# A two-layer streaming trunk on one core: the pair preparation of layer 1 with the value projection one pair ahead

## What is computed

```python
k = xk @ w_k
v = xv @ w_v
kk = heads(k * k_k)
kk = kk / jnp.maximum(jnp.sqrt(jnp.sum(kk * kk, axis=-1, keepdims=True)), L2_EPS)
k_mod = k.astype(f32) * (1.0 + (a - 1.0) * k_a.astype(f32))
b_h = kk * a_h
# the scan over tokens uses r, decay, k_mod, v, kk and b; afterwards
o = o + (jnp.sum(r_h * k_h * r_k, axis=-1, keepdims=True) * v_h).reshape(B, T, D_MODEL)
```

## Time and profile before

| What | us |
|---|---|
| median of the three runs (4078.36 to 4090.19) | 4087.38 |
| the profiled execution | 4082.8 |
| its span, first to last instruction | 4081.0 |
| the pair stage in it: last key tile read (2153.4) to L1932 (2350.0) | 196.6 |

### The profile page before, as it was taken

The page is one execution under the profiler, slowest core; times in us unless marked ns, Lnnn a source line. Parts: engine busy times, 40 slices in busy tenths (PEclk is TensorE's granted clock), DMA queues, the critical chain, the costliest instruction groups (busy, mean ns, idle before and its releaser), DMA issues.

```text
span 4081.0 us, 65997 instructions
## 1 busy us (share of the span) xinstructions
PE 3684.9 (90%) x28466; PEld 3299.1 (81%) x28466; DVE 1534.3 (38%) x2023; ACT 853.4 (21%) x1132; POOL 206.8 (5%) x347
## 2 busy tenths in 40 slices
PE   6999999799999998968997768888698999999977
PEld 4997348699999997844996657777497999999967
DVE  3134544522212224431337734454625221222352
ACT  2001322300000001133324423333422000001020
POOL 0000000000000000000002111111100000000000
PEclk8999999899999999986998878898899999999989
DMA  2222011111121131112325732121412112112111
GB/s 88 67 68 79 21 42 71 65 47 41 57 75 47 42 128 39 39 61 109 113 86 217 269 107 54 43 54 29 145 37 75 41 40 76 63 41 99 66 37 70
DMA packets 75366, 300.53 MB, mean 74 GB/s; under 512 B 9400, under 2 KB 11720, under 8 KB 71160
## 3 DMA queue, kind: packets, MB, share of 16 engines
q0 software_dynamic: 36816, 174.51, 11.7%
q1 hardware_dynamic: 38336, 122.87, 9.6%
HBM read 216.24 MB, written 81.10 MB: 73 GB/s over the span
## 4 chain that ended last, share of the span: by engine, by line
PE 72%; DVE 8%; issue 2%; ACT 2%; DMA 1%; POOL 0%; DVEq 0%; ACTq 0%; POOLq 0%
PE ps L447 54%; PE ps L421 3%; DVE A L1470 2%; PE ps L856 2%; PE ps L847 2%; PE ps L757 1%; DVE B L1470 1%; PE ps L461 1%; PE ps L807 1%; DVE H L1551 1%; DVE A_r L1527 1%; PE ps L870 1%; PE ps L873 1%; PE ps L479 1%; PE ps L822 1%
## 5 line engine op out<-in xcount | busy, mean ns | idle before, releaser
L447 PE MATMUL ps<-H_r,W_r 128*128 128x364 f32 (+1 forms) x3192 | 705.2, 329 | 0.0
L447 PE MATMUL ps<-H_r,TM_r 128*128 128x364 f32 x2736 | 606.7, 330 | 21.7 <-DVE A_r L1527 18.2
L447 PE MATMUL ps<-A_r,TM_r 128*128 128x364 f32 x2736 | 606.2, 330 | 0.0
L447 PEld LDWEIGHTS ps<-H_r,W_r 128*128 128x128 f32 (+1 forms) x3192 | 555.9, 188 | 1.8
L447 PEld LDWEIGHTS ps<-H_r,TM_r 128*128 128x128 f32 x2736 | 475.1, 189 | 28.2 <-issue 19.8
L447 PEld LDWEIGHTS ps<-A_r,TM_r 128*128 128x128 f32 x2736 | 476.8, 189 | 0.0
L447 PE MATMUL ps<-B_r,DW_r 128*128 128x364 f32 x2112 | 408.9, 329 | 0.0
L447 PE MATMUL ps<-B_r,W_r 128*128 128x364 f32 x1824 | 405.0, 330 | 0.0
L447 PEld LDWEIGHTS ps<-B_r,DW_r 128*128 128x128 f32 x2112 | 358.8, 188 | 0.0
L447 PEld LDWEIGHTS ps<-B_r,W_r 128*128 128x128 f32 x1824 | 319.7, 190 | 0.0
L1733 DVE TENSOR_TENSOR TM<-ps,TM 128x1092 f32<-128x1092 f32 x44 | 57.0, 1296 | 444.4 <-PE ps L447 444.4
(11 more groups left out here) (288 smaller groups left out, 4390.2 us busy)
## 6 DMA issues: line engine op xcount, KB each, us to landing
W<-in_wgu SPq DMA_DIRECT2D x88, 512.0 KB, 3.6
H<-d_h POOLq DMA_DIRECT2D x3, 4368.0 KB, 23.0
W<-in_wdown SPq DMA_DIRECT2D x32, 384.0 KB, 3.1
W<-in_wrkv SPq DMA_DIRECT2D x24, 512.0 KB, 3.6
W<-in_wdown SPq DMA_DIRECT2D x32, 320.0 KB, 2.9
d_h<-H POOLq DMA_DIRECT2D x16, 546.0 KB, 3.0
d_y<-TM POOLq DMA_DIRECT2D x16, 546.0 KB, 3.4
A<-d_y POOLq DMA_DIRECT2D x16, 546.0 KB, 7.9
```

The lines of the kernel that those rows point to most:

```text
L447: ins = nc.tensor.matmul(ps[0:cols, NCH * s + c, 0:CH], w[:, j * cols:(j + 1) * cols], x[k1][:, c * CH:(c + 1) * CH], start=(k1 == 0 and n ...
```

## The change

The pair loop is written out (it was a loop of two times four pairs), and five things in it differ.

1. TensorE runs V one pair ahead: V(0), then for each pair A(p), V(p+1), R(p).
2. ScalarE squares the next key (`key_square(pair + 1)`, which waits for that pair's four loads) and then takes V(p+1) out of PSUM (`value_tile(pair + 1)`), and then R(p).
3. The upper part of the value weights is made by ScalarE (`upper_value`), two pairs ahead; VectorE only subtracts (`lower_value`). The scaling by `ka` moves to ScalarE as well, into `tmpK`.
4. VectorE's clamp of A(p) is gone: the logarithm reads PSUM directly with a tiny bias, and the normed key takes a minimum with 1/L2_EPS. The scaling of the log decay is folded into the scale of the exponentials.
5. GpSimd stores v one pair ahead: `keep_value(0)`, then in iteration p `keep_value(p + 1)` ahead of the store of the sum.

The core of the diff:

```diff
-                    sums(k("pair"), TM[:, 1, :])
-                    split_unit(xh, xlow[1])
-                    pe.wait_ge(S["rk_ready"], t.up("rk_ready"))
-                    sums(k("pair"), TM[:, 2, :])
+            split_unit(xh, xlow[1], arriving=True)
+            for pair in range(NPAIR):
+                pe.wait_ge(S["key_sq"], pair + 1)
+                sums(k("pair"), TM[:, 1, :])
+                if pair + 1 < NPAIR:
+                    split_unit(xh, xlow[1])
+                pe.wait_ge(S["rk_ready"], pair + 1)
+                sums(k("pair"), TM[:, 2, :])
...
+            def key_square(pair):
+                key, L = key2[pair % 2], Lb[pair % 2]
+                if pair >= 2:
+                    act.wait_ge(S["pair_done"], pair - 1)
+                act.wait_ge(S[f"l_in{pair % 2}"], t.up(f"l_in{pair % 2}", 64))
+                nc.scalar.activation(key, L["k"], ACT.Copy, scale=v1("kk", pair)).then_inc(S["key_scaled"], 1)
+                act.wait_ge(S["key_scaled"], pair + 1)
+                nc.scalar.activation(TM[:, 1, :], key, ACT.Square).then_inc(S["key_sq"], 1)
...
+            upper_value()
+            upper_value()
+            key_square(0)
+            value_tile(0)
+            for pair in range(NPAIR):
...
+                nc.scalar.activation(tmpK, L["a"], ACT.Identity, scale=v1("ka", pair),
+                                     bias=kab[:, pair:pair + 1]).then_inc(S["k_scale"], 1)
...
+                nc.scalar.activation(c3(TM[:, 3, :]), pset(s), ACT.Ln, bias=eps[:, 2:3]).then_inc(S[f"read{s}"], 1)
...
+                nc.scalar.activation(L["w"], L["w"], ACT.Exp, scale=-DECAY).then_inc(S["act_p"], 1)
+                if pair + 2 < NPAIR:
+                    upper_value()
+                if pair + 1 < NPAIR:
+                    key_square(pair + 1)
+                    value_tile(pair + 1)
+                s, mm, rd = t.unit()
+                act.wait_ge(S["mm_done"], mm)
+                nc.scalar.activation(c3(TM[:, 2, :]), pset(s), ACT.Copy).then_inc(S[f"read{s}"], 1)
...
+                nc.vector.tensor_tensor_scan(cumL, reset, L["w"], 0.0, ALU.mult, ALU.add).then_inc(S["dve_p"], 1)
+                nc.vector.tensor_tensor(L["w"], cumL, L["w"], ALU.subtract).then_inc(S["dve_p"], 1)
+                nc.vector.tensor_tensor(L["k"], tmpK, L["k"], ALU.mult).then_inc(S["k_used"], 1)
+                stt(TM[:, 2, :], L["r"], v1("rk", pair), L["k"], ALU.mult, ALU.mult).then_inc(S["rk_ready"], 1)
+                stt(key, TM[:, 3, :], 1.0 / L2_EPS, key, ALU.min, ALU.mult).then_inc(S["rn_used"], 1)
...
+            keep_value(0)
+            for i in range(NPAIR):
+                t.skip(1)
+                if i + 1 < NPAIR:
+                    keep_value(i + 1)
                 s, mm, rd = t.unit()
                 pool.wait_ge(S[f"read{s}"], rd)
                 pool.dma_start(d_x["sum"][i], TM[:, 2, :]).then_inc(S["sum_out"], 16)
```

More of the change, by code:

```diff
@@ L55 @@
 DECAY = float(np.exp(-0.5))
+TINY = 1e-34
 SUMS = 8
@@ L315, in build_trunk @@
[L315 to L318, removed]
@@ L1313, in _ @@
             act.wait_ge(S["xn_ready"], t.val("xn_tmp"))
[L1314 to L1349, removed]
@@ new lines, in lower_value @@
+            def lower_value(pair):
+                slot, landed = t.chunk()
+                dve.wait_ge(S["vh_ready"], pair + 1)
+                nc.vector.tensor_tensor(Wr[:, slot, 0:KT * P], W[:, slot, 0:KT * P], wh_of(t),
+                                        ALU.subtract).then_inc(S["wl_ready"], 1)
+                t.up("wl_ready")
+            tmpK = DWf[:, 0:T]
+            lower_value(0)
+            lower_value(1)
+            for pair in range(NPAIR):
+                key, L = key2[pair % 2], Lb[pair % 2]
+                dve.wait_ge(S[f"l_in{pair % 2}"], t.up(f"l_in{pair % 2}", 64))
+                nc.vector.tensor_tensor_scan(cumL, reset, L["w"], 0.0, ALU.mult, ALU.add).then_inc(S["dve_p"], 1)
+                dve.wait_ge(S["dve_p"], t.up("dve_p"))
+                nc.vector.tensor_tensor(L["w"], cumL, L["w"], ALU.subtract).then_inc(S["dve_p"], 1)
+                t.up("dve_p")
+                dve.wait_ge(S["k_scale"], pair + 1)
+                dve.wait_ge(S["key_scaled"], pair + 1)
+                nc.vector.tensor_tensor(L["k"], tmpK, L["k"], ALU.mult).then_inc(S["k_used"], 1)
+                dve.wait_ge(S["k_used"], pair + 1)
+                dve.wait_ge(S["sum_stored"], t.up("sum_stored"))
+                stt(TM[:, 2, :], L["r"], v1("rk", pair), L["k"], ALU.mult, ALU.mult).then_inc(S["rk_ready"], 1)
+                t.up("rk_ready")
+                dve.wait_ge(S["key_rn"], t.up("key_rn"))
+                stt(key, TM[:, 3, :], 1.0 / L2_EPS, key, ALU.min, ALU.mult).then_inc(S["rn_used"], 1)
+                dve.wait_ge(S["rn_used"], t.up("rn_used"))
+                step(nc.vector.tensor_tensor(tmpA, key, L["a"], ALU.mult))
+                dve.wait_ge(S["pair_stored"], t.up("pair_stored"))
+                dve.wait_ge(S["act_p"], t.up("act_p", 2))
+                for dst, x, y in zip(chunks(ar_out, o=C), tokens(L["r"]), tokens(expL)):
+                    nc.vector.tensor_tensor(dst, x, y, ALU.mult)
+                for dst, x, y in zip(chunks(bk_out), tokens(tmpA), tokens(expnL)):
+                    nc.vector.tensor_tensor(dst, x, y, ALU.mult)
+                for dst, x, y in zip(chunks(bk_out, o=C), tokens(L["k"]), tokens(expnL)):
+                    nc.vector.tensor_tensor(dst, x, y, ALU.mult)
+                dve.wait_ge(S["act_p"], t.up("act_p"))
+                if pair + 2 < NPAIR:
+                    lower_value(pair + 2)
+                for dst, x, y in zip(chunks(ar_out), tokens(key), tokens(L["w"])):
+                    ins = stt(dst, x, -1.0, y, ALU.mult, ALU.mult)
+                ins.then_inc(S["pair_done"], 1)
+                dve.wait_ge(S["pair_done"], t.up("pair_done"))
@@ L2231, in _, with keep_value @@
             pool.sem_inc(S["pair_stored"], 1)
-            for i in range(NPAIR):
-                t.skip(1)
+            def keep_value(i):
                 s, mm, rd = t.unit()
```

103 lines of the change are left out of this document (47 added, 56 removed).

## The result

The changed kernel takes 4065.46 us (median; 4060.14 to 4069.30) against 4087.55 of the kernel before beside it (4078.36 to 4092.07): ratio 0.9947, 95% interval 0.993 to 0.9963. It is 22 us faster; 9 us slower was predicted.

A forecast was written before the change was run, and what follows sets the result against it. TensorE's chain bounds the pair stage now, 21.17 us per pair; after the change, load landings gate it: 2217 + 5 × 22.6 = 2330, plus 29.0 gives L1932 at 2359, +9 on 4087.4 = 4096 us; range 4082 to 4108.

The forecast's parts named there:

- the sum: Whole kernel: L1932 starts at 2359 against 2350.0, so +9 us on 4082.8, or 4096 us against the median.
- The case "faster": Pair stage: loads in before ScalarE asks, TensorE sets the pace at 15.7 us a pair, −41 us, 4046; chance 0.08.
- The cycle: Pair stage: one pair's load landing gates issue of the next pair's loads; 8.9 us plus d_bk's issue to last landing.
- the waits named as signs: Pair stage: ScalarE waits longest for loads, TensorE about 5 us ahead of A, VectorE for `pair_stored`; d_bk to d_bk 22 to 24.
- The start of the cycle: Pair stage entry: d_bk(0) at 2204, pair 2's loads landed 13 later at 2217, against 2209.5 today.
- X: Pair stage: time from d_bk's issue to the last load's landing, taken as 13.7 us; 13.0 without the weight load.
- the period: Pair stage: time from one pair's load landing to the next's, 22.6 us, 1.4 more than today; bounds 21.9 and 24.7.
- the weight load's hour: Pair stage: weight load issued 7.5 to 8.1 us after a pair's loads land (L), ahead of d_bk at L + 8.9.
- The first rival: Pair stage: weight load still collides in full, period 24.0 to 24.7, +16 to +19 us, 4103 to 4106; chance 0.32.
- The end: Pair stage's end: after pair 7's loads land no further load follows; L1932 starts 29.0 us after that landing.
- The work taken off VectorE: Pair stage: clamp, scaling and cast leave VectorE, some 3.0 to 3.4 us a pair; booked as zero gain.
- The offer of 40 us: Pair stage: TensorE's 21.2 us a pair less 15.7 of work, 5.5 a pair, some 40 us if nothing else becomes late.

The follow-up runs named there:

- experiments 1 and 3: Kernel before with only TensorE's pair loop written out, 4039.09 us; kernel before with 128 unused semaphore increments on TensorE between pair stage and scan, 4032.78 us.
- Experiment 4: Changed kernel with ScalarE squaring the next key after taking V of the next pair and R out of PSUM: 4042.09 us, ratio 0.9909.
- experiment 10: Changed kernel with the key's load put ahead of the stores d_bk and d_ar, with its own semaphore that the squared key waits for: 4031.21 us, ratio 0.9880.
- Experiment 7: Changed kernel with SyncE holding each weight load of the pair stage until a pair's loads have landed: 4052.64 us, ratio 0.9947.
- experiment 12: Changed kernel with the key loaded first, plus 221 unused semaphore increments on TensorE between the stages: 4023.01 us, ratio 0.9856.

## Why the prediction was wrong, point by point

- **The step that failed is the sum.** "+9 us on the profiled execution's 4082.8" carries everything outside the pair stage over unchanged, without a reason given. It was not: the scan gave back 44.7 us, and experiments 1 and 3 show that this came from the number of TensorE instructions ahead of it, with the pair stage as before: the stops for instructions fell from 24 to 6, and the time at the lower clock from 92 to 24 us. No rival named it. The case "faster", 0.08, had another mechanism that did not happen.
- **The cycle was right.** The landing of one pair's loads gates the issue of the next pair's; the waits named as signs are those of the changed kernel (d_bk to d_bk is 24.2 us, just above the 22 to 24 named). Experiment 4 takes the key from ahead of the tiles and 19.4 of the 20.7 us are gone; experiment 10 leaves the order and lets the key land early, and the stage falls below that of before.
- **The start of the cycle was right.** d_bk(0) was put at 2204; it is issued at 2210.12, in a stage that began 5.7 later. Pair 2's loads landed at 2224.0, so 2218.3 counted from the old start, where 2217 was said.
- **X was mis-sized,** 13.7 against 15.0, and with it the period, 22.6 against 24.3. The forecast called the weight load's hour rightly (L + 7.9, 1.0 us ahead of d_bk) and took that for half out of the way. The load did get out of the way itself, landing after 3.8 us, but the last load behind it still came 15.0 after d_bk. Experiment 7, with it wholly out of the way, has X at 14.2: the value "without it 13.0" subtracted both a slow stretch and the load's own bytes from 15.1, 2.1 us in all, of which 0.9 is borne out. The sum's store to d_bk took 4.5, not 3.8, and from the landing to that store 4.8, not 5.2; these two nearly cancel.
- **The first rival had the size:** +16 to +19 for the stage; it is +20.7, with X above its point of 14.4. But the weight load beside the stores is 7.3 of it (experiment 7), not the whole.
- **The end** was 31 us after the last landing, not 29: d_bk(7) was issued 12.7 us after d_bk(6) (2356.26 and 2368.98), as forecast, but d_bk(6) came 10.6 after the landing and not 8.9.
- **The work taken off VectorE was rightly booked at zero.** It is busy 132.5 instead of 155.3 us in the stage, and with the old order of the key (experiment 4) the stage is as long as before.
- **The offer of 40 us was real in part.** Experiment 10's order brings 10 to 12 of it and experiment 12, the same code in the stage, 14 to 16.

What stays open is why a packet comes late behind some matmuls and in time behind others. Fewer stops and a higher clock came together in every good run: over the scan the clock is 0.89 to 0.92 at places 0 and 64, 0.94 to 0.95 at 127 to 162. The order within the traces puts the stop first and the fall of the clock behind it; no run changes the one without the other.

## What to carry to other kernels

Divide the two traces into stages before reading any of them: a stage with the same instructions and another length says that the edit acted through something other than that stage's work; here it was the instruction stream. An edit that changes how many instructions stand ahead of a long loop of short matmuls should be timed at two or three numbers of idle instructions, or else a gain or a loss of 1% may be put down to the wrong part. And an operation that waits for a transfer belongs behind those on its engine that let the next transfer go, unless that transfer is made to land early.

## What the runs showed of the hardware

128 semaphore increments on TensorE, ahead of a loop of 5152 instructions that does not change, make this loop's stage 53 us of 544 shorter, and 256 give nothing; half of the 16 KB that the instruction queue moves in one packet is the best of the four places tried. TensorE's stops for nothing else that the profile shows lie at the packets' boundaries, and end mostly 2.2 to 2.8 us after a packet has started. Writing the loop out made the stage 27 us longer, though the two jumps were gone; the boundaries had moved. The granted clock went with it, from 0.89 to 0.95 over half a millisecond, with the same matmuls.
